# The depthwise convolution block of a two-part transformer kernel: the order of its taps, its squares and its first output tile

## The reference

```
a, gate = split(x @ w_pw1 + b_pw1)          # 1024 -> 2 x 1024
h = a * sigmoid(gate)
h = depthwise_conv(h, w_dw, width 31, 15 zeros on each side) + b_dw
mu, var = mean and variance of h over the channels
h = silu((h - mu) / sqrt(var + 1e-5) * ln_g + ln_b)
out = h @ w_pw2 + b_pw2
```

## Time and profile before

| | us |
|---|---|
| median of 3 runs | 2700.09 |
| lowest and highest run | 2699.97, 2705.06 |
| the profiled execution, its own time | 2704.8 |
| its span in the trace | 2702.8 |

### The profile page before, as it was taken

How to read it: one execution, slowest core, us unless ns; L and a number is a source line. 1 busy time by engine, 2 the same in 40 slices (tenths; PEclk the granted TensorE clock), 3 DMA queues, 4 the chain that set the end, 5 groups by cost and what they waited for, 6 DMA issues and landing times.

```text
span 2702.8 us, 37579 instructions
## 1 busy us (share of the span) xinstructions
PE 2649.8 (98%) x14653; PEld 2119.0 (78%) x14653; DVE 1546.5 (57%) x2261; ACT 1001.2 (37%) x1414; POOL 359.6 (13%) x330
## 2 busy tenths in 40 slices
PE   7999999999999999999999999999999999999999
PEld 5787878787777768888888888888888764888887
DVE  6666756676666664444635444654444776645445
ACT  4544446356655542222342222332222313422223
POOL 1110101021000021111121111121112121211110
PEclk8999999999999999999979999999999999999999
DMA  3222222132222213222212322222322452222231
GB/s 115 81 82 75 78 64 94 39 103 71 78 70 78 78 48 109 93 93 93 93 47 94 105 97 93 93 94 96 106 93 94 119 159 56 94 94 93 98 104 62
DMA packets 171509, 238.23 MB, mean 88 GB/s; under 512 B 6513, under 2 KB 149371, under 8 KB 171411
## 3 DMA queue, kind: packets, MB, share of 16 engines
q1 hardware_dynamic: 163523, 217.23, 24.4%
q0 software_dynamic: 6080, 19.43, 2.6%
q10 hardware_dynamic: 1808, 0.21, 0.1%
HBM read 232.36 MB, written 4.40 MB: 88 GB/s over the span
## 4 chain that ended last, share of the span: by engine, by line
PE 88%; DVE 6%; ACT 2%; DMA 2%; issue 1%; POOL 1%; DVEq 0%; ACTq 0%; POOLq 0%
PE ps L382 20%; PE ps L384 20%; PE ps L383 20%; PE ps L795 5%; PE ps L797 4%; PE ps L796 4%; DVE w_lo L359 1%; DVE probs L1722 1%; PE ps L368 1%; PE ps L369 1%; PE ps L370 1%; PE ps L1574 1%; DMA glu_scratch<-glu 1%; PE ps L1585 1%; PE ps L2072 1%
## 5 line engine op out<-in xcount | busy, mean ns | idle before, releaser
L354 ACT ACTIVATE w_hi<-w_raw 128x2048 fp32r<-128x2048 f32 x203 | 388.5, 1914 | 889.4 <-PE ps L384 882.6
L382 PE MATMUL ps<-h_hi,w_hi 128*128 128x512 f32 x1456 | 567.7, 390 | 1.2 <-DVE w_lo L359 1.2
L384 PE MATMUL ps<-h_hi,w_lo 128*128 128x512 f32 x1456 | 566.6, 389 | 0.0
L383 PE MATMUL ps<-h_lo,w_hi 128*128 128x512 f32 x1456 | 566.4, 389 | 0.0
L359 DVE TENSOR_TENSOR w_lo<-w_raw,w_hi 128x2048 fp32r<-128x2048 f32 x203 | 464.8, 2290 | 130.8 <-ACT w_hi L354 130.8
L427 DVE SCALAR_TENSOR_TENSOR xT<-ps,xT 128x512 f32<-128x512 f32 x488 | 325.6, 688 | 137.1 <-PE ps L384 136.2
L382 PE MATMUL ps<-a_hi,w_hi 128*128 128x512 f32 x992 | 386.3, 389 | 5.3 <-issue 3.5
L384 PE MATMUL ps<-a_hi,w_lo 128*128 128x512 f32 x992 | 385.9, 389 | 0.0
L383 PE MATMUL ps<-a_lo,w_hi 128*128 128x512 f32 x992 | 385.9, 389 | 0.0
L1807 POOL TENSOR_TENSOR f_gate<-f_gate,n_rstd 128x512 f32<-128x512 f32 x88 | 176.9, 2012 | 1123.8 <-ACT f_gate L1801 1123.8
L382 PEld LDWEIGHTS ps<-h_hi,w_hi 128*128 128x128 f32 x1456 | 273.3, 188 | 60.6 <-issue 2.5
(11 more groups left out here) (346 smaller groups left out, 2928.4 us busy)
## 6 DMA issues: line engine op xcount, KB each, us to landing
w_raw<-in_ffn_w_in_dram SPq DMA_DIRECT2D x88, 1024.0 KB, 5.0
w_raw<-in_ffn_w_out_dram SPq DMA_DIRECT2D x44, 1024.0 KB, 4.8
w_raw<-in_a_w_in_dram SPq DMA_DIRECT2D x24, 1024.0 KB, 5.3
w_raw<-in_b_w_in_dram SPq DMA_DIRECT2D x16, 1024.0 KB, 5.4
w_raw<-in_conv_w_pw_dram SPq DMA_DIRECT2D x12, 1024.0 KB, 5.6
shifted<-glu_scratch POOLq DMA_DIRECT2D x32, 264.0 KB, 4.6
w_raw<-in_a_w_out_dram SPq DMA_DIRECT2D x8, 1024.0 KB, 4.8
w_raw<-in_b_w_out_dram SPq DMA_DIRECT2D x8, 1024.0 KB, 4.8
```

Of the source, the lines that this page charges most:

```text
L354: nc.scalar.activation(w_hi[:, t % 2], w_raw[:, t % 2], ACT.Copy).then_inc(hi_done, 1)
L382: nc.tensor.matmul(dst, wh, xh, start=(k == 0), stop=False)
L383: nc.tensor.matmul(dst, wh, xl, start=False, stop=False)
L384: m = nc.tensor.matmul(dst, wl, xh, start=False, stop=last)
```

## The change

- TensorE's loop: value tile and gate tile of pair i+1, and then the taps of pair i, each of its two blocks with waits of its own. After the loop the sums of `dw_y` for blocks 0 to 3, one `pe_warm`, and the taps of pair 3, block by block ahead of sums 4 and 5; then one `pe_warm` and sums 6 and 7.
- VectorE's loop over the pairs is written out, with fixed addresses. The 22 taps of a pair are cut in thirds of 6, 10 and 6 instructions; the addition of TensorE's taps of pair i-1 stands between the thirds. The first split of an iteration stands at its start as before, the second behind the taps instead of among them.
- GpSimd issues both stores of a pair first. The shifted copies of a block are issued behind the wait for `taps_done` and ahead of its `tap_blocks`.
- ScalarE issues a one-column Ln ahead of the squares. The squares use four buffers. TensorE sums squares 0 to 3; VectorE adds 4 to 5 and 6 to 7 (p0, p1), and TensorE sums these two. Six `pe_warm` follow instead of eight.
- The first "O" tile (`pe_first_out`): for output blocks 0 to 3 first the three products of input block 0, as soon as its low part is there (`pw2_half`), and then those of input block 1. VectorE adds the output blocks 0 and 1 right behind the split of the next tile, and 2 and 3 behind the next pair's low parts.

The diff, cut: bodies that the kernel above shows are left out where they are only removed.

```diff
@@ -2052,26 +2052,27 @@
...
 glu_moved = [sem("glu_moved0"), sem("glu_moved1")]
-glu_stored = sem("glu_stored")
+glu_stored = [sem("glu_stored0"), sem("glu_stored1")]
+pw2_half = sem("pw2_half")
...
 ln_pe = Marks(sem("ln_pe"), ["sum"])
-ln_dve = Marks(sem("ln_dve"), [f"c{n}" for n in range(KC)] + [f"n{n}" for n in range(KC)])
+ln_dve = Marks(sem("ln_dve"), [f"c{n}" for n in range(KC)] + ["p0", "p1"] + [f"n{n}" for n in range(KC)])
 ln_act = Marks(sem("ln_act"), [f"s{n}" for n in range(KC)])
-def pe_taps(pe, i=None):
...
+def pe_taps(pe, c, i=None):
+    last = KC // 2 - 1
+    pe.wait_ge(taps_added, 2 * last + c + 1 if i is None else i * 2 + (c + 1))
+    pe.wait_ge(diag_ready, 2 * last + c + 1 if i is None else i * 2 + (c + 1))
+    pe.wait_ge(glu_moved[c], (last + 1) * GLU_MOVES if i is None else i * GLU_MOVES + GLU_MOVES)
+    for j in range(PE_STEPS):
+        for g, r in enumerate(ROWS):
+            ins = nc.tensor.matmul(ps[r, 4 + c], tap_blocks[:, c, g * PE_STEPS + j],
+                                   shifted[:, c, g, j * SHIFTS:j * SHIFTS + T], start=j == 0, stop=j == PE_STEPS - 1)
+    ins.then_inc(taps_done, 1)
...
     for k in range(NC):
@@ -2079,28 +2080,63 @@
...
         pe_tile(pe, t, i, NC, between=lambda: pe.wait_ge(in_free, at(in_before, t, i, NC) + IN_CREDIT))
-        pe_taps(pe, i)
         pe_tile(pe, t + 1, i, NC)
+        pe_taps(pe, 0, i)
+        pe_taps(pe, 1, i)
     in_all_free(pe, T_PW2)
     for n in range(KC):
-        if n == 0:
-            pe_warm(2, 2)
-            pe.wait_ge(taps_added, KC)
+        if n in (KC - 4, KC - 3):
+            if n == KC - 4:
+                pe_warm(1, 2)
+            pe_taps(pe, n - (KC - 4))
         elif n == KC - 2:
-            pe_warm(4, 2)
-            pe_taps(pe)
             pe_warm(1, 2)
-            pe.wait_ge(taps_added, KC + 2)
+        pe.wait_ge(taps_added, n + 3 if n >= KC - 4 else KC - 2)
...
-    for n in range(KC):
+    for n in range(4):
         pe.wait_ge(sq_ready, 8 * m + n + 1)
-        nc.tensor.matmul(ps[:, 6], ones[:], n_sq[:, n % 2], start=n == 0, stop=n == KC - 1
-                         ).then_inc(sum_ready if n < KC - 1 else stat_ready, 1)
-    pe_warm(8, 2)
-    for s in range(4):
+        nc.tensor.matmul(ps[:, 6], ones[:], squares[n], start=n == 0, stop=False).then_inc(ln_summed, 1)
+    for n in range(2):
+        ln_dve.wait(pe, f"p{n}")
+        ins = nc.tensor.matmul(ps[:, 6], ones[:], squares[2 * n], start=False, stop=n == 1)
+    ins.then_inc(stat_ready, 1)
+    pe.sem_inc(sum_ready, KC - 1)
+    pe_warm(6, 2)
+    pe_first_out(pe)
+    for s in range(1, 4):
         pe_tile(pe, T_PW2 + s)
+squares = [n_sq[:, 0], n_sq[:, 1], n_h[:, 0], n_h[:, 1]]
+ln_summed = sem("ln_summed")
+def pe_first_out(pe):
+    t = T_PW2
+    pe.wait_ge(lo_done, t + 1 + SPLIT_CREDIT)
+    wh, wl, buf = w_hi[:, t % 2], w_lo[:, t % 2], pairs_before(t) % 2
+    def half(n, k):
+        w, dst = slice(k * D + n * P, k * D + n * P + P), ps[:, 4 + n % 4]
+        nc.tensor.matmul(dst, wh[:, w], a_hi[:, buf, k], start=k == 0, stop=False)
+        nc.tensor.matmul(dst, wh[:, w], a_lo[:, buf, k], start=False, stop=False)
+        ins = nc.tensor.matmul(dst, wl[:, w], a_hi[:, buf, k], start=False, stop=k == 1)
+        if k == 1:
+            ins.then_inc(chunk_done, 1)
+    pe.wait_ge(out_free, out_before(t) + OUT_CREDIT)
+    pe.wait_ge(ln_logs, 1)
+    pe.wait_ge(pw2_half, 1)
+    for n in range(4):
+        half(n, 0)
+    pe.wait_ge(pair_ready, pairs_before(t) + 1)
+    for n in range(4):
+        half(n, 1)
+    for n in range(4, 8):
+        pe.wait_ge(out_free, out_before(t) + (n - 4 + OUT_CREDIT + 1))
+        half(n, 0)
+        half(n, 1)
...
@@ -2114,23 +2150,18 @@
...
         for c in range(2):
+            pool.wait_ge(in_free, in_before(T_PW1 + 2 * i) + 2 * c + 2 + IN_CREDIT)
+            pool.dma_start(glu_scratch[2 * i + c], glu[:, 2 * i + c]).then_inc(glu_stored[c], 16)
+        for c in range(2):
             pool.wait_ge(taps_done, i * 2 + (1 + c))
+            pool.wait_ge(glu_stored[c], 16 * i + 16)
+            for u, to in enumerate(ROWS):
+                src = glu_scratch[2 * i + c, :, u:u + T + PE_TAPS - SHIFTS]
+                pool.dma_start(shifted[to, c], src.rearrange("(g q) t -> q g t", g=4)).then_inc(glu_moved[c], 16)
...
                                     tap, ALU.mult).then_inc(diag_ready, 1)
-        for c in range(2):
...
     t = T_PW1 + base
@@ -2148,7 +2179,14 @@
...
         act_glu(act, NC, i)
-    act_squares(act, m, lambda e, n: ln_dve.wait(e, f"c{n}"), dw_y)
+    nc.scalar.activation(table_junk[:], eps[:, 0:1], ACT.Ln).then_inc(junk_ready, 1)
+    for n in range(KC):
+        ln_dve.wait(act, f"c{n}")
+        if n >= 4:
+            act.wait_ge(ln_summed, n - 3)
+        elif n < 2:
+            act.wait_ge(stat_ready, m)
+        nc.scalar.activation(squares[n % 4], dw_y[:, n], ACT.Square).then_inc(sq_ready, 1)
...
     act.wait_ge(ln_logs, 1)
@@ -2192,44 +2230,26 @@
...
-def dve_taps(dve, i=None, t=None):
+def dve_taps(dve, i, taps):
     v = nc.vector
-    if t is not None:
...
+    dve.wait_ge(in_free, in_before(T_PW1 + NC + 2 * i) + IN_CREDIT)
+    for j in taps:
         for c in range(2):
-            n = KC - 2 + c
-            y = dw_y[:, n:n + 1] if i is None else dw_y[:, bass.ds(i * 2 + c, 1)]
-            src = (glu[:, n:n + 1] if i is None else glu[:, bass.ds(i * 2 + c, 1)])[:, :, j:j + T]
-            tap = pc(PARAMS["dw"] + j * KC + c)
+            y, src = dw_y[:, 2 * i + c], glu[:, 2 * i + c, j:j + T]
+            tap = col("dw", j * KC + 2 * i + c)
             if j == PE_TAPS:
-                ins = v.tensor_scalar(y, src, tap, pc(PARAMS["dw_b"] + c), ALU.mult, ALU.add)
+                ins = v.tensor_scalar(y, src, tap, col("dw_b", 2 * i + c), ALU.mult, ALU.add)
             else:
-                done = 2 * (j - PE_TAPS) + c - 1
-                dve.wait_ge(dw_step, before * DW_STEPS + done if i is None else i * DW_STEPS + done)
+                dve.wait_ge(dw_step, i * DW_STEPS + 2 * (j - PE_TAPS) + c - 1)
...
-def dve_taps_add(dve, i=None):
...
+def dve_taps_add(dve, i, c):
+    dve.wait_ge(dw_step, i * DW_STEPS + DW_STEPS - 1 + c)
+    dve.wait_ge(taps_done, 2 * i + c + 3)
+    nc.vector.tensor_tensor(dw_y[:, 2 * i + c], dw_y[:, 2 * i + c], ps[:, 4 + c], ALU.add).then_inc(taps_added, 1)
...
     v = nc.vector
@@ -2239,30 +2259,50 @@
...
     dve_glu(dve, 0)
-    with dve.Fori(0, KC // 2 - 1) as i:
...
+    third = (DW - PE_TAPS) // 3
+    for i in range(KC // 2):
+        t = T_PW1 + NC + 2 * i
+        if i < KC // 2 - 1:
+            split_tile(dve, t + 1)
+        dve_taps(dve, i, range(PE_TAPS, PE_TAPS + third))
+        if i:
+            dve_taps_add(dve, i - 1, 0)
+        dve_taps(dve, i, range(PE_TAPS + third, DW - third))
+        if i:
+            dve_taps_add(dve, i - 1, 1)
+        dve_taps(dve, i, range(DW - third, DW))
+        if i < KC // 2 - 1:
+            split_tile(dve, t + 2)
+            dve_glu(dve, NC + 2 * i)
+    dve_taps_add(dve, KC // 2 - 1, 0)
+    dve_taps_add(dve, KC // 2 - 1, 1)
...
         ln_dve.done(f"c{n}", v.scalar_tensor_tensor(dw_y[:, n], ps[:, 0], -1.0 / D, dw_y[:, n], ALU.mult, ALU.add))
+    for n in range(2):
+        dve.wait_ge(sq_ready, 8 * m + 2 * n + 6)
+        ln_dve.done(f"p{n}", v.tensor_tensor(squares[2 * n], squares[2 * n], squares[2 * n + 1], ALU.add))
...
         scaled(n)
-    dve_pair(dve, T_PW2, dw_y[:, 0:2])
+    buf = pairs_before(T_PW2) % 2
+    for d in range(2):
+        dve.wait_ge(a_hi_ready, 2 * pairs_before(T_PW2) + d + 1)
+        v.tensor_tensor(a_lo[:, buf, d], dw_y[:, d], a_hi[:, buf, d].bitcast(F32), ALU.subtract
+                        ).then_inc((pw2_half, pair_ready)[d], 1)
+    scaled(4)
     split_tile(dve, T_PW2 + 1)
-    scaled(4)
+    add_chunks(dve, T_PW2, (0, 1))
     scaled(5)
     dve_pair(dve, T_PW2 + 1, dw_y[:, 2:4])
+    add_chunks(dve, T_PW2, (2, 3))
...
     for s in range(3):
-        add_chunks(dve, T_PW2 + s, range(0 if s == 0 else 2, 8))
+        add_chunks(dve, T_PW2 + s, range(4 if s == 0 else 2, 8))
...
             dve_pair(dve, T_PW2 + s + 2, dw_y[:, 2 * s + 4:2 * s + 6])
```

More of the change, by code:

```diff
@@ L2060, in build @@
         ln_pe = Marks(sem("ln_pe"), ["sum"])
-        ln_dve = Marks(sem("ln_dve"), [f"c{n}" for n in range(KC)] + [f"n{n}" for n in range(KC)])
+        ln_dve = Marks(sem("ln_dve"), [f"c{n}" for n in range(KC)] + ["p0", "p1"] + [f"n{n}" for n in range(KC)])
         ln_act = Marks(sem("ln_act"), [f"s{n}" for n in range(KC)])
-        def pe_taps(pe, i=None):
-            pe.wait_ge(taps_added, KC if i is None else i * 2 + 2)
-            for c in range(2):
[L2068 to L2074, removed]
+        def pe_taps(pe, c, i=None):
[8 more added lines that the diff above has]
+            ins.then_inc(taps_done, 1)
         def pe_conv(pe, m, q):
@@ L2121, in gp_taps @@
                                             tap, ALU.mult).then_inc(diag_ready, 1)
```

(36 more changed lines are left out.)

## The result

The changed kernel took 2682.69 us (median of 5 runs, 2677.13 to 2688.49) against 2702.38 us for the kernel before on the same chip. The ratio is 0.9925, with a 95% interval of 0.9909 to 0.9941: faster by 20.3 us, between 15.9 and 24.6. The forecast was 14.7 us, with a time of 2685.4. The profiled execution took 2688.49 us, where 2690.1 was forecast for it; its span is 2686.7, which is 16.1 less than before. Two of the five runs lie near 2677, two near 2687 and one between; the last experiments say where that comes from.

What follows compares the result with a forecast made beforehand. TensorE's own work bounds the loop, a chain of hand-overs the block's end. Gains 10.2 (loop 2.4, tail 7.8) + 1.4 + 3.1 = 14.7 us, from 2700.09 to 2685.4; range 2680.5 to 2692.5.

Steps and rivals of the forecast that it cites:

- The loop: Convolution loop over the pairs: TensorE's three waits for shifted copies go, winning 2.4 us, between 1.5 and 2.7.
- A loop's end behind taps: Each loop end now follows taps instead of a tile: 0 to 0.4 us allowed for each, 0.1 taken.
- a gap: TensorE's idle time between a pair's two tap blocks in the loop: 0.79 us, plus some 0.1 of lost overlap each.
- The tail: Loop's end to VectorE's first subtraction: 18.1 us instead of 25.9, so 7.8 us nearer.
- The three things that had to be ready: Behind the loop: pair 3's shifted copies, VectorE's taps and additions, and an unfallen clock; no wait taken, bound 0.5 us.
- X: Start of VectorE's subtractions behind the convolution block, forecast 10.2 us earlier, bounds 8.5 to 10.7.
- X to the Ln: From VectorE's first subtraction to the layer norm's Ln: 7.85 us instead of 9.24, 1.4 us gained, bounds 0.5 to 2.
- The output tile: First output tile: starts 3.6 us behind `n_rstd`, takes 11.3; 3.1 us gained by early start and stall, bounds 1.5 to 3.5.
- The rule on the Exp's table: Rival, 6%: one set serves Ln and Exp, so Exp's load goes, 1.3 us less, 2684.1; forecast followed the trace instead.
- The clock: Rival, 8%: the clock falls ahead of the first output tile, costing about 3 us, 2688.4.
- VectorE as the bound: Rival, 3%: written-out taps take over 0.97 us each in the loop, so VectorE bounds it; at 1.33 each, 2724 us.
- 5 us upward: Allowance for run spread over the whole kernel, from runs like 2705.06 beside 2699.97, giving range 2680.5 to 2692.5.

Runs made afterwards that it cites:

- the last experiments: Changed kernel with a shorter tail (0.9925 of the kernel before), with two more dummies in the pooling (0.9905), and with both edits (0.9877, median 2674.43 us).
- The three kernels with an idle time of 2.5 us or more ahead of the tile: Changed kernel with old squares and old first output tile (block 173.95 us), old first tile only (170.87), or no dummies ahead of the tile (169.56).
- each of two parts alone: Changed kernel with the squares as before (block 169.01 us), and changed kernel with the first output tile as before (170.87), against 167.55 for the changed kernel.
- both together: Changed kernel with both the squares and the first output tile as before: block 173.95 us, ratio 0.9957 to the kernel before.

## Why the prediction was right

- **The loop.** The mechanism was right, the size a little off: 3.1 us won instead of 2.4, above my bound of 2.7. Two terms were mis-sized. A loop's end behind taps was allowed 0.1 us and cost nothing that can be seen: from the taps' start to the next tile's start it is 8.72 us (2167.59 to 2176.31), which is the two blocks alone. And a gap cost 0.2 us beyond its idle time and not 0.1: the taps of the three pairs, from their start to the next tile's, took 9.5, 9.9 and 9.7 us, 2.9 more than three times 8.72, of which 2.3 were idle time. The last 0.2 us of the 3.1 lie in the tiles.
- **The tail.** 18.1 us were forecast and 18.1 measured, since the list is gapless and could be summed from its pieces. The three things that had to be ready were ready: the copies (block 0 landed at 2241.53, wanted at 2242.30), VectorE and the clock. The run with GpSimd's old order shows that this readiness was the point: X is then only 0.6 us earlier than before the change. The prediction named GpSimd's part, but gave it no price of its own. One bound of it was wrong: copies were to land within 6.5 us of their issue, and in the changed loop one took 10.7. There it was covered (landed at 2164.19, wanted near 2171.9); in the tail, where 0.8 us were left, the longest of block 0 took 6.0.
- **X to the Ln.** It is 7.78 us against a forecast of 7.85. The early Ln was rightly counted at nothing; without it the Ln came at the same time.
- **The output tile.** It started 3.7 us behind `n_rstd` and was 11.1 long, against a forecast of 3.6 and 11.3. VectorE's additions were in time.
- **The rule on the Exp's table.** The load of 1.28 us is at 2264.43, between Ln and Exp, as before, though the Ln's set had been loaded early. Here the rule of the Trainium skill that one set serves both ("ScalarE: Activation LUTs", "Table sets: the hidden batching unit") did not hold, and the trace decided rightly.
- **The clock.** It didn't fall at the output tile (1.00). The three kernels with an idle time of 2.5 us or more ahead of the tile had it fall in the tile.
- **VectorE as the bound.** It wasn't, and the kernel before with VectorE alone written out was unchanged. But the row of 0.67 us for a tap doesn't hold everywhere: two or three taps of each pair took 1.2 to 2.7 us, all of them while GpSimd computed `tap_blocks`. A pair's 22 taps took 16.8 to 17.5 us, where the sum had 16.9 with its allowance of 2 x 1.1.
- **The rest of the 20 us.** 15.7 us of the difference are the block, one more than the 14.7 of the sum (0.7 in the loop, 0.3 in the two last parts). The medians differ by more because two of five runs of the changed kernel lay near 2677, while of 17 runs of before beside the first experiments only 2 lay near 2692. I had not foreseen that and had put the spread down to 5 us upward. What decides whether a run has the second fall in the pooling isn't shown, so that part of the 20 us is luck for the forecast, and the block is the better test of the sum.

## What to carry to other kernels

When a list of work on the bounding engine can be made gapless, its time is the sum of its pieces, and the question is only whether each operand is there in time: work that out per operand, with the worst landing time. The engine that feeds it (here GpSimd with a store and its copies) must be reordered with it: with its old order 10.3 of 10.9 us were gone. Undo the parts one at a time but also together: each of two parts alone was undone at its own price, and both together cost 1.65 us more, for the clock.
